# A routed mixture-of-experts layer: the router's logits formed per token tile, expert ranks summed on TensorE, combine weights computed beside the gather, and the low token parts subtracted on VectorE

## The reference

```python
def hierarchical_moe(h, router_group_w, router_group_b, router_expert_w, router_expert_b, ...):
    grp_logits = (xf @ router_group_w) + router_group_b           # 4 groups
    grp = jnp.argmax(grp_logits, axis=-1)
    grp_w = softmax(grp_logits)[grp]
    exp_logits = (xf @ router_expert_w) + router_expert_b         # 4 groups x 8 experts
    exp_logits = exp_logits[group grp]
    top_p, top_j = lax.top_k(softmax(exp_logits), 2)
    combine = grp_w * top_p / jnp.sum(top_p)
    # every token goes to two of the 32 experts:
    #   hid = silu(xb @ w_gate[e]) * (xb @ w_up[e]);  y = hid @ w_down[e]
    #   output = sum over its two experts of combine * y
```

## Time and profile before

| | |
|---|---|
| time, median of 3 runs | 2248.48 us (2247.1 to 2249.78) |
| the profiled execution | 2246.21 us |
| its span, first to last instruction | 2244.4 us |
| granted TensorE clock, mean over the span | 0.970 of full speed |
| PE busy | 2090.6 us, 93% of the span |
| DVE busy | 1040.2 us, 46% |
| ACT busy | 372.2 us, 17% |
| POOL busy | 141.1 us, 6% |
| moved by DMA | 484.17 MB, 216 GB/s on the mean |

### The profile page before, as it was taken

The page is one execution under the profiler, slowest core; times in us unless marked ns, Lnnn a source line. Parts: engine busy times, 40 slices in busy tenths (PEclk is TensorE's granted clock), DMA queues, the critical chain, the costliest instruction groups (busy, mean ns, idle before and its releaser), DMA issues. The chain is left out here.

```text
span 2244.4 us, 25036 instructions
## 1 busy us (share of the span) xinstructions
PE 2090.6 (93%) x9444; PEld 1197.5 (53%) x9445; DVE 1040.2 (46%) x1741; ACT 372.2 (17%) x736; POOL 141.1 (6%) x61
## 2 busy tenths in 40 slices
PE   5999999999689999999779999999995999999994
PEld 2437888854245555554244488888443454445541
DVE  5896433342424444433378953343424333334433
ACT  2203232300201111111021032332001011111111
POOL 0001212100100000000000022120001000000000
PEclk9999999999899999999979999999997999999997
DMA  5111111124259999999451011112142799999993
GB/s 214 58 46 39 56 54 41 60 109 156 112 228 420 422 423 422 421 421 422 188 204 48 19 57 57 38 57 76 75 156 113 329 420 420 422 420 423 423 423 134
DMA packets 68353, 484.17 MB, mean 216 GB/s; under 512 B 8992, under 2 KB 9504, under 8 KB 46496
## 3 DMA queue, kind: packets, MB, share of 16 engines
q1 hardware_dynamic: 68256, 482.89, 52.9%
HBM read 476.58 MB, written 6.29 MB: 215 GB/s over the span
## 5 line engine op out<-in xcount | busy, mean ns | idle before, releaser
L1427 DVE TENSOR_TENSOR x_tokens<-x_tokens,ps 128x512 f32<-128x512 f32 x256 | 172.0, 687 | 245.9 <-PE ps L775 245.0
L791 PE MATMUL ps<-slabs,arena 128*64 128x512 f32 x512 | 225.3, 593 | 4.0 <-issue 3.6
L791 PE MATMUL ps<-arena 128*64 128x512 f32 x512 | 225.0, 592 | 2.6 <-DVE arena L1417 2.6
L841 PE MATMUL ps<-slabs,branch 128*64 128x512 f32 x512 | 226.6, 595 | 0.0
L841 PE MATMUL ps<-arena,branch 128*64 128x512 f32 x512 | 226.6, 595 | 0.0
L792 PE MATMUL ps<-slabs,arena 128*64 128x512 f32 x512 | 225.9, 594 | 0.0
L792 PE MATMUL ps<-arena 128*64 128x512 f32 x512 | 225.0, 592 | 0.0
L604 PE MATMUL ps<-h_hi,w_parts 128*128 128x512 f32 x768 | 209.5, 407 | 0.0
L459 PE MATMUL ps<-slabs,hT 128*128 128x512 f32 x384 | 174.2, 615 | 9.1 <-DVE hT L1332 7.5
L1523 POOL TENSOR_TENSOR w_parts<-slabs,w_parts 128x2048 fp32r<-128x2048 f32 x24 | 110.9, 4622 | 684.8 <-ACT w_parts L939 684.8
L604 PEld LDWEIGHTS ps<-h_hi,w_parts 128*128 128x128 f32 x768 | 140.1, 192 | 25.1
(11 more groups left out here) (288 smaller groups left out, 3125.8 us busy)
## 6 DMA issues: line engine op xcount, KB each, us to landing
arena<-in_expert_w_gate SPq DMA_DIRECT2D x32, 2048.0 KB, 14.5
arena<-in_expert_w_up SPq DMA_DIRECT2D x32, 2048.0 KB, 18.9
arena<-in_expert_w_down SPq DMA_DIRECT2D x32, 2048.0 KB, 11.6
slabs<-in_expert_w_gate SPq DMA_DIRECT2D x32, 2048.0 KB, 17.2
slabs<-in_expert_w_up SPq DMA_DIRECT2D x32, 2048.0 KB, 21.7
slabs<-in_expert_w_down SPq DMA_DIRECT2D x32, 2048.0 KB, 16.3
slabs<-in_dense SPq DMA_DIRECT2D x18, 2048.0 KB, 8.2
slabs<-in_gate_w SPq DMA_DIRECT2D x24, 1024.0 KB, 4.8
```

Of the source, the lines that this page charges most:

```text
L791: nc.tensor.matmul(ps[0:64, BANK_GU[b], :], xk, low[:, k, :], start=(k == 0), stop=(k == ND - 1), tile_position=(0, 0))
L841: done = nc.tensor.matmul(ps[64 * b:64 * b + 64, BANK_Y[half], :], hidT[:, k, CAP * b:CAP * (b + 1)], w_down[b][:, k, half * 512:(half + 1 ...
L1427: v.tensor_tensor(xs, xs, ps[:, BANK_BACK[n % 2], :], ALU.add).then_inc(s["back_added"], 1)
```

## The change

- `hT` of the tail goes to a buffer of its own, `h2T`, in the place of `xe`. So ACT no longer waits for the logits before it writes `x_hi`; it waits for the last output product and for each tile's `xn`.
- The logits are formed per tile as `h2T[tile].T @ rw`, tokens on partitions, directly in the wanted form. `route_logits(0)` stands in the tail after the transposes of tile 1, `route_logits(1)` after those of tile 2, the other two at the end. The copy to `logitT` and the turn back are gone.
- `x_lo` is computed on DVE, between the last `take_transposed` and the bias addition. POOL has no work there any more.
- `sel_all` follows the one-hot choices directly. DVE sums the selections of earlier tiles (`before`), and PE adds triangle times `sel_all` and ones times `before` in one PSUM accumulation: the rank over all tokens. `slot` is then one instruction, (rank + 1) * `sel_all`, compared with `iota` + 1.
- `gtmp` and the difference `e2` come after the sums; the combine weights and the counts are computed after `build_sel(0)`.
- PE no longer waits for `route_done` before the gather nor for both halves of `xe` before the first gate product (the gate products wait for the half that they read). ACT no longer waits for `route_done`.

```diff
+        h2T = view(A - 4 - 2 * ND * QUAD, ND, S)
...
+                    def route_logits(t):
+                        pe.wait_ge(s["proj_free"], J_TAIL + TAIL.index(("h", t, 1)) + 1)
+                        if t == 0:
+                            pe.wait_ge(s["router_in"], 16 * (ND + 1))
+                        for k in range(ND):
+                            last = nc.tensor.matmul(ps[:, BANK_S[0], t * 36:(t + 1) * 36], h2T[:, k, t * P:(t + 1) * P], rw[:, k, :],
+                                                    start=(k == 0), stop=(k == ND - 1))
+                        last.then_inc(s["rt_done"], 1)
...
                             transpose_x(J_TAIL + n, t, half)
-                    pe.wait_ge(s["proj_free"], J_END)
-                    pe.wait_ge(s["router_in"], 16 * (ND + 1))
-                    for k in range(ND):
-                        last = nc.tensor.matmul(ps[0:36, BANK_S[0], :], rw[:, k, :], hT[:, k, :], start=(k == 0), stop=(k == ND - 1))
-                    last.then_inc(s["rt_done"], 1)
-                    pe.wait_ge(s["rt_read"], 1)
-                    for t in range(NT):
-                        last = nc.tensor.matmul(ps[:, BANK_S[1], t * 36:(t + 1) * 36], logitT[:, t * P:(t + 1) * P], ident[:, 0:36],
+                            if half == 1 and t >= 1:
+                                route_logits(t - 1)
+                    route_logits(NT - 1)
...
-                    nc.tensor.matmul(ps[:, BANK_T[0], 0:P], tri, flat, start=True, stop=True)
-                    last = nc.tensor.matmul(ps[:, BANK_T[1], 0:P], ones, flat, start=True, stop=True)
-                    last.then_inc(s["rank_done"], 1)
+                    nc.tensor.matmul(ps[:, BANK_T[0], 0:P], tri, flat, start=True, stop=False)
+                    pe.wait_ge(s["earlier_ready"], 1)
+                    nc.tensor.matmul(ps[:, BANK_T[0], 0:P], ones, before.rearrange("p t e -> p (t e)"), start=False, stop=True)\
+                      .then_inc(s["rank_done"], 1)
...
-                    pe.wait_ge(s["route_done"], 1)
...
-                    pe.wait_ge(s["xe_ready"], 2)
...
-                    act.wait_ge(s["rt_done"], 1)
+                    act.wait_ge(s["proj_done"], J_TAIL + TAIL.index(("mix", NT - 1, 1)) + 1)
                     for t in range(NT):
+                        act.wait_ge(s["xn_ready"], NT + t + 1)
                         nc.scalar.activation(x_hi[:, t, :], xn[:, t, :], ACT.Identity).then_inc(s["x_hi_ready"], 1)
...
+                    for t in range(NT):
+                        dve.wait_ge(s["x_hi_ready"], t + 1)
+                        v.tensor_tensor(x_lo[:, t, :], xn[:, t, :], x_hi[:, t, :], ALU.subtract).then_inc(s["x_lo_ready"], 1)
...
+                    link(v.tensor_scalar(iota, iota, 1.0, None, ALU.add))
+                    link(v.memset(before[:, 0], 0.0))
...
+                    tell(v.tensor_tensor(sel_all, oh[0], oh[1], ALU.add), "sel_ready")
+                    link(v.tensor_copy(before[:, 1], sel_all[:, 0]))
+                    link(v.tensor_tensor(before[:, 2], before[:, 1], sel_all[:, 1], ALU.add))
+                    tell(v.tensor_tensor(before[:, 3], before[:, 2], sel_all[:, 2], ALU.add), "earlier_ready")
+                    tell(v.tensor_tensor(em[:, 0, :], before[:, 3], sel_all[:, 3], ALU.add), "count_in")
+                    tell(v.tensor_tensor(gtmp, gl, gmax.unsqueeze(2).to_broadcast([P, NT, 4]), ALU.subtract), "gexp_in")
                     tell(v.tensor_tensor(e2, top2, top1, ALU.subtract), "e2_in")
...
+                    link(v.scalar_tensor_tensor(slot.rearrange("p e t -> p t e"), ps[:, BANK_T[0], 0:P].rearrange("p (a b) -> p a b", a=NT),
+                                                1.0, sel_all, ALU.add, ALU.mult))
...
-                    for t in range(NT):
-                        pool.wait_ge(s["x_hi_ready"], t + 1)
-                        g.tensor_tensor(x_lo[:, t, :], xn[:, t, :], x_hi[:, t, :], ALU.subtract).then_inc(s["x_lo_ready"], 1)
```

More of the change, by code:

```diff
@@ L1006, in _ @@
                     nc.scalar.activation(table_in, ident[:, 0:1], ACT.Identity).then_inc(s["table_in"], 1)
-                    act.wait_ge(s["route_done"], 1)
                     def pair(i, first):
@@ L1064, in normalise, with take_transposed @@
                         tell(v.tensor_scalar(to, of, rstd[:, one], None, ALU.mult), "xn_ready")
-                    def take_transposed(n, t, half, g):
+                    def take_transposed(n, t, half, g, hT=hT):
                         dve.wait_ge(s["proj_done"], n + 1)
@@ L1374, in _ @@
                     one_hot(goh, gl, gmax, desc4, 4, first)
-                    tell(v.tensor_tensor(gtmp, gl, gmax.unsqueeze(2).to_broadcast([P, NT, 4]), ALU.subtract), "gexp_in")
                     link(v.tensor_scalar(goh, goh, 1.0, -NEG, ALU.subtract, ALU.mult))
@@ L1382, in _ @@
                     one_hot(oh[1], em, top2, desc32, 32, first)
-                    tell(v.tensor_tensor(e2, top2, top1, ALU.subtract), "e2_in")
-                    tell(v.tensor_tensor(sel_all, oh[0], oh[1], ALU.add), "sel_ready")
-                    dve.wait_ge(s["gexp_done"], 1)
-                    link(v.tensor_reduce(gden, gtmp, AX, ALU.add))
-                    dve.wait_ge(s["e2_done"], 1)
-                    link(v.tensor_scalar(den1, e2, 1.0, None, ALU.add))
-                    link(v.tensor_tensor(den1, den1, gden, ALU.mult))
@@ L1390, in _ @@
-                    link(v.reciprocal(cw[0], den1))
-                    link(v.tensor_tensor(cw[1], cw[0], e2, ALU.mult))
-                    for k in range(2):
-                        link(v.tensor_tensor((em, eq)[k], oh[k], cw[k].unsqueeze(2).to_broadcast([P, NT, 32]), ALU.mult))
-                    link(v.tensor_tensor(wtab.rearrange("p e t -> p t e"), em, eq, ALU.add))
-                    link(v.memset(before[:, 0], 0.0))
-                    dve.wait_ge(s["rank_done"], 1)
-                    tot = ps[:, BANK_T[1], 0:P].rearrange("p (a b) -> p a b", a=NT)
@@ L1398, in _ @@
-                    link(v.tensor_copy(before[:, 1], tot[:, 0]))
-                    for t in range(1, NT):
-                        to = before[:, t + 1] if t < NT - 1 else countf[:, 0:N_EXP]
-                        link(v.tensor_tensor(to, before[:, t], tot[:, t], ALU.add))
-                    link(v.scalar_tensor_tensor(eq, ps[:, BANK_T[0], 0:P].rearrange("p (a b) -> p a b", a=NT), 1.0, before,
-                                                ALU.add, ALU.add))
-                    link(v.tensor_tensor(eq, eq, sel_all, ALU.mult))
@@ L1406, in _ @@
-                    link(v.tensor_scalar(slot[:, 0:N_EXP, :].rearrange("p e t -> p t e"), eq, -1.0, None, ALU.add))
-                    link(v.tensor_reduce(countf[:, N_EXP:N_EXP + 1], countf[:, 0:N_EXP], AX, ALU.max))
-                    tell(v.tensor_copy(counts, countf), "route_done")
+                    tell(v.tensor_tensor(sel_all, oh[0], oh[1], ALU.add), "sel_ready")
+                    link(v.tensor_copy(before[:, 1], sel_all[:, 0]))
+                    link(v.tensor_tensor(before[:, 2], before[:, 1], sel_all[:, 1], ALU.add))
@@ L1474, in _ @@
                     build_sel(0)
+                    dve.wait_ge(s["gexp_done"], 1)
+                    link(v.tensor_reduce(gden, gtmp, AX, ALU.add))
+                    dve.wait_ge(s["e2_done"], 1)
+                    link(v.tensor_scalar(den1, e2, 1.0, None, ALU.add))
+                    link(v.tensor_tensor(den1, den1, gden, ALU.mult))
+                    link(v.reciprocal(cw[0], den1))
+                    link(v.tensor_tensor(cw[1], cw[0], e2, ALU.mult))
+                    dve.wait_ge(s["rank_done"], 2)
+                    link(v.tensor_copy(countf[:, 0:N_EXP], ps[:, BANK_T[1], 0:N_EXP]))
+                    for k in range(2):
+                        link(v.tensor_tensor((em, eq)[k], oh[k], cw[k].unsqueeze(2).to_broadcast([P, NT, 32]), ALU.mult))
+                    link(v.tensor_tensor(wtab.rearrange("p e t -> p t e"), em, eq, ALU.add))
+                    link(v.tensor_reduce(countf[:, N_EXP:N_EXP + 1], countf[:, 0:N_EXP], AX, ALU.max))
+                    tell(v.tensor_copy(counts, countf), "route_done")
                     for half in range(2):
```

20 lines of the change are left out of this document (9 added, 11 removed).

## The result

The changed kernel takes 2227.17 us, the median of 4 runs (2223.35 to 2228.52), against 2248.59 before (4 runs, 2247.1 to 2249.78): a ratio of 0.990, 95% interval 0.989 to 0.992. It is 21.4 us faster, where 30.9 were forecast. The profiled execution took 2228.21 us (span 2226.4).

The account below looks back on a forecast made before the run. The expert stage was taken as bound by its transfers, its start by the routing chain. Gains of 4.06 + 7.28 + 2.79 + 1.32 = 15.45 us per layer, twice 30.9, gave 2217.5 us, range 2211 to 2224.

Parts of the forecast that it names:

- Tail: Tail before routing: tile 0's logits go ahead of the last output product and cost 2.1 us per layer.
- From the last copy to the bias addition: Start of routing: bias addition 5.22 us after the last copy instead of 11.38, copy 2.1 later; gain 4.06 per layer.
- Choice of experts: Bias addition to the end of `sel_all`: 5.78 us instead of 13.06 without POOL beside it; gain 7.28 per layer.
- rival of slow small operations: Choice of experts: 16-number operations slow by themselves, not because of POOL; 6.6 us per layer, 2230.8; chance 0.04.
- Ranks: From `sel_all` to `build_sel`: 1.77 us instead of 4.56; gain 2.79 per layer.
- Selection matrix to the load: Gather to gate products: PE's idle wait for the second `take` goes; gain 1.32 us per layer.
- the rival of an earlier full clock: Gather: starts at full clock or gets it earlier; 2.1 us per layer more gained, 2213.4; chance 0.07.
- The logits end last: Before the bias addition: at half clock the last logits end 0.85 us after DVE, or 3.85; 2219.3 to 2225; chance 0.10.
- PE stays at half clock: Tail through gate products: clock stays down, 25.4 us against 15.45 gained, 10 lost per layer, 2268; chance 0.02.
- Its signs of being wrong: DVE waiting over 1 us for PE before the bias addition, longer slow gather, or gaps in expert-stage transfers.
- its end follows its start: Expert stage: as long as its 449 us of transfers, so an earlier start ends it equally earlier.
- The rival of an earlier start that is not kept: Expert stage: held by something besides its transfers, so half the gain might go; 2233 us; chance 0.03.

Follow-up runs that it names:

- slots 8 and 148: Changed kernel, TensorE's layer-loop code begun at instruction 8 or 148 of a 256-instruction fetch block: 2217.7 and 2220.54 us at 8, 2216.51 us at 148.
- (kernel before): Kernel before the change, TensorE's layer-loop code begun 74 instructions later in a fetch block: 2252.65 us against 2247.17, ratio 1.002.
- long overflow code, two places: Changed kernel, gather in the never-entered overflow code standing twice, TensorE's loop begun at block instruction 8 or 148: 2220.36 and 2216.67 us.
- slot 78 and its own place, shortened: Changed kernel, overflow gather cut to one of eight chunks: 2223.42 us with TensorE's loop entered by a jump at block instruction 78, 2227.7 us without the jump.
- slot 8, lengthened: Changed kernel, TensorE's loop begun at block instruction 8, gather in the never-entered overflow code standing twice: 2220.36 us.

## Why the prediction was wrong

**Right:** that the chain is on the path, and nearly all its terms, in the sum 32.2 us instead of 30.9. That the sum came so close is in part luck: layer 1 gained 14.35 us and layer 2 17.87, against 15.45 forecast for each, and in the ten profiles with the changed kernel's work the two layers gain 29.3 to 35.3 together against the profile of before, by where the clock falls.

- *Tail.* 1.87 us for the first logits, 1.74 and 1.53 by the last copy (2.1 forecast). The low parts took 4.62 (4.87). From the last copy to the bias addition, tail included, 3.59 and 5.62 gained (4.06). ScalarE's four roundings all came behind the norm of tile 3 (593.59 to 597.47), not three beside it; that cost nothing.
- *Choice of experts.* 5.77 us, forecast 5.78; its cause shown by the run that moved the low parts alone on the kernel before. The rival of slow small operations fell with it.
- *Ranks.* 2.05 us (1.77). *Selection matrix to the load*: 0.95 and 2.43 gained (1.32). The idle time ahead of the gate products went in both layers; the slow part of the gather grew in layer 1, from 4.9 to 6.06 us, and in layer 2 the clock came back after 3.3 us, which is the rival of an earlier full clock, in one layer.
- *The logits end last.* This rival, given 0.10, came true in layer 1, 1.25 us late, as its case at half clock had it (0.85); in layer 2 of the first profile VectorE was last. Over the ten profiles with this work the logits end last in 13 of 20 layers (bias addition 6.05 us behind the last copy) and VectorE in 7 (4.84). *PE stays at half clock* did not come true: the clock rose in the gather.
- *Its signs of being wrong.* Two of three appeared, VectorE's wait for TensorE above 1 us and the longer slow part of the gather, yet they cost the chain little. The third, gaps in the transfers, did not: 1.01 of their time is busy, as before.

**Wrong:** the sum's closing step. From "its end follows its start" it took all that lies behind expert 2's load at the times of before, and "frees nothing else" was the only look it had at the rest of the program. The term for TensorE's longer code was thereby put at nothing, without a reason. In its place the runs showed a branch of 3.80 and 3.93 us instead of 0.35, layers' ends 3.0 and 3.3 us longer, and expert stages 2.8 and 1.1 us longer, although the transfers did keep step (the last one is issued 433 us behind expert 2's load in every profile). In its own place the changed kernel takes 2227 to 2228.5; at slots 8 and 148, the same work takes 2216.5 to 2220.5 (four series with the branch short and the up matrix on time), on both sides of the 2217.5 forecast. The rival of an earlier start that is not kept (2233) came nearest in kind, since a part of the loss is in the expert stage; but it named no cause, and the larger part lies behind that stage.

Of the 14.2 us lost in the first profile, the branch is shown: 6.3 us in the rows. In medians it gave 5.5 us (kernel before), 3.7 (long overflow code, two places), 0.9 and 0.8 (slot 78 and its own place, shortened), and 2.7 or nothing (slot 8, lengthened). So the rows are sure and the median's share is not: the clock in other stretches moves by as much (the chain between its two forms, 4.84 and 6.05 us behind the last copy; the expert stage between 470.5 and 473.9). That a faster branch is partly paid back by the clock behind it, and not by chance, is not excluded. The later landing is shown to vanish with the place or with the jump; with it the expert stage is 1 to 3 us longer, the most where the clock drops too. Why it lands late is not settled. The rest, 3.7 us in layer 1's mixer, is wander.

The version to keep is the changed kernel with the layer loop at slot 148 or 8: 2216.5 us, and 2217.7 and 2220.5, some 7 to 12 us under the change as it was made.

## What to carry to other kernels

When a change makes an engine's instruction stream longer, count where its taken branches come to stand against the fetched blocks, above all those that all engines wait behind; a branch over cold code is such a place even though nothing of it runs. Cut the span of both kernels at the same few events before looking for a cause: here 32 us of gain and 14 of loss stood in different rows, and the net said neither. And when two producers end close together, find out which one ends last before taking work from the other: here it was TensorE at half clock in 13 of 20 layers, and there a VectorE without its subtractions started the bias addition no earlier.

## What the runs showed of the hardware that was not expected

- TensorE's branch past code that is not entered took 0.34 to 0.35 us where no instruction fetch fell into it, and 3.3 to 3.9 where one did, in every profile. The loop's branch back to its head takes 3.3 to 4.1 us in every kernel; TensorE's first product of layer 2 starts 5 us behind its end, waiting for VectorE, so nobody waits there.
- 16 records of the 128x36 products take 1.87 us at a granted clock of 1.00 (2.4 GHz) and 3.63 at 0.50 (1.2 GHz).
- The up matrix of expert 31 lands 23.0 to 23.5 us after its issue in the four profiles in the changed kernel's own place, and 21.9 to 22.5 in all others, one of which differs from the changed kernel by nothing but the jump into TensorE's loop.
